# Two transformer blocks on one core: the ends, the passage between the blocks, the pooling products and the order of an FFN's last step rearranged

## The chip, the cores and the metric

The kernel runs on one core of one Trainium2 chip. The metric is the device time of one execution in microseconds (us). The change is judged by the medians of several executions of the two kernels on the same chip.

## What is computed

An input `x` of 256 tokens by 1024 features passes through two stacks of two layers each. All weights are float32.

```python
def first_block(x, mem, ...):
    for l in range(DEPTH):                       # DEPTH = 2
        x = x + 0.5 * swiglu(rms_norm(x, ffn1_norm[l]), ffn1_w_gate[l], ffn1_w_up[l], ffn1_w_down[l])
        x = x + hybrid_mixer(rms_norm(x, mix_norm[l]), w_in[l], ...)
        x = x + memory_cross_attention(rms_norm(x, cross_norm[l]), rms_norm(mem, mem_norm[l]), ...)
        x = x + 0.5 * swiglu(rms_norm(x, ffn2_norm[l]), ...)
    return rms_norm(x, final_norm)

def second_block(x, ...):
    for l in range(DEPTH):
        x = x + swiglu_half(rmsnorm(x, g_ffn1[l]), w1_ffn1[l], w3_ffn1[l], w2_ffn1[l])
        h = rmsnorm(x, g_mix[l])
        q_sb, k_sb, v_sb, q_r, k_r, v_r, g_r, u_p, gate = jnp.split(h @ w_in[l], split_points, axis=-1)
        y_sb, y_ret = stick_breaking_attention(q_sb, k_sb, v_sb), retention(q_r, k_r, v_r, g_r)
        y_pool = pool_mixer(u_p, w_pool[l], pool_scale[l])
        merged = gates[:, :, 0] * (y_sb @ w_branch_sb[l]) + gates[:, :, 1] * (y_ret @ w_branch_ret[l]) \
            + gates[:, :, 2] * (y_pool @ w_branch_pool[l])
        x = x + merged @ w_out[l]
        x = x + swiglu_half(rmsnorm(x, g_ffn2[l]), w1_ffn2[l], w3_ffn2[l], w2_ffn2[l])
    return rmsnorm(x, g_final)
```

`swiglu(h) = (silu(h @ w_gate) * (h @ w_up)) @ w_down` with 2816 hidden features. The kernel writes the 256x1024 result as its only output.

## The kernel before

**Split products.** A float32 product is made of three passes in the float32r format. Every weight tile is split by ScalarE (ACT) into a rounded part `whi` (`split_hi`) and by VectorE (DVE) into the rest `wlo` (`split_lo`); the activations, transposed on TensorE (PE) against the identity matrix `ident` (`turn_piece`), are split in the same way into `hT_hi` and `hT_lo` (`turn_out` on ACT and on DVE). `split_product` then issues three matmuls.

**Units.** All weights pass as 1 MB units through a ring of three slots (`raw`, `whi`, `wlo`). SyncE (SP) loads unit u+3 into a slot once DVE has made `wlo` of unit u; ACT rounds unit u+3 once PE has finished unit u. One such unit is 24 matmuls with 512 columns (or their like), so PE, DVE and ACT move through the program in step, each in its own written order. The order of every engine is written out by hand, with semaphores between them.

**The FFN.** `ffn` works in 11 steps of 256 hidden features: two units of gate and up weights, one unit of down weights. The first step is made for tokens as rows (`tokens_unit`), the following by `wide_unit`; the last `down` uses `last_aT`. In the last step ACT rounds the next stage's first unit (`off + FFN_UNITS`) before it evaluates silu and rounds the product. The FFN's result is added to the residual `xres` in four pieces (piece i is token half i % 2 and feature half i // 2) by DVE: `add_and_norm` adds a piece (`add`), multiplies it with the gain of the next norm (`gained`, giving `xn`), and in between makes the rests of the first two transposed pieces (`turn_out`) that the next stage's first unit needs. There are eight FFNs; after seven of them such a stage follows.

**Norms.** The reciprocal root of the mean square is applied later, so the squares (`squares` on ACT, then a root on ACT and a reciprocal on DVE) run beside the next stage's first products. Between the blocks there are two norms one behind the other: `gain_final`, `joint_squares` and `final_scale` compute both, while the products already run on `x` times both gains.

**Branches of block 1.** Behind the 22 units of `w_in_2` PE transposes the retention output of each token half (`r_yT`), and between the two does the small products of the pooling mixer with `w_pool` (`pool_groups`, into PSUM bank 2). ACT and DVE turn that result into a split operand (`p_hi`, `p_lo`). Before the first branch unit (`B_BR`, stick-breaking) PE waits for `s_lo` and for `p_lo`:

```python
pe.wait_ge(s_lo, l + 1)
pe.wait_ge(p_lo, l + 1)
tall_unit(1, l, B_BR, from_hT(0), 0, True, True)
```

DVE multiplies each branch output with its gates; for the last branch (units `B_BR + 2` and `+ 3`) this goes by pieces, and the pieces of `xn` feed the output projection `B_OUT`.

**Ends.** At the start the ACT queue loads a gain row, two pieces of `x`, `ident`, two more pieces; SP loads the first unit in two halves and then whole units. PE spreads the gain row over 128 partitions by two matmuls (one bank of 512 columns each), DVE multiplies (`first_piece`), PE transposes, and the first unit begins. At the end `last_output` (DVE) and `last_norm` (ACT) make the final norm; DVE scales all four pieces, and the last is stored from the ACT queue.

## Time and profile before

| | |
|---|---|
| time, median of 3 executions | 2411.71 us (2410.25 to 2413.52) |
| the profiled execution's own time | 2411.78 us |
| its span, first to last instruction | 2410.0 us |
| TensorE busy | 2387.7 us, 99% of the span, 13060 matmul records |
| TensorE weight loads busy | 2056.7 us, 85% |
| VectorE, ScalarE, GpSimd busy | 1541.1, 1198.1, 66.4 us |
| HBM read | 425.60 MB, 177 GB/s over the span |
| mean granted TensorE clock | 0.999 |

Busy time of TensorE is that of pipelined matmuls whose ends are modelled: it tells where PE is not idle, and the spacing of the starts tells the speed. The granted clock is 1.00 at 2.4 GHz and 0.50 at 1.2 GHz. For the first microseconds the column prints 1.00 although the spacing of the matmuls is that of the lower level; there the spacing tells the level.

### The profile page before, as it was taken

How to read it: one execution, taken by the hardware profiler on the slowest of the kernel's cores; microseconds unless marked ns; L12 is line 12 of the kernel's file. 1: busy time of each engine (PE TensorE's matmuls, PEld its weight loads, DVE VectorE, ACT ScalarE, POOL GpSimd, SP SyncE). 2: the span in 40 equal slices, each digit the busy share in tenths (PEclk: the TensorE clock that was granted, in tenths of full speed). 3: DMA queues.
4: the chain of work that ended last, by engine and by line, in shares of the span. 5: the costliest groups of instructions: out<-in, count | busy, mean ns of one | idle time of the engine just before them, and what ended most of it. 6: DMA issues, size and time to landing. Idle time of an engine off the chain costs nothing.

```text
span 2410.0 us, 33389 instructions
## 1 busy us (share of the span) xinstructions
PE 2387.7 (99%) x13060; PEld 2056.7 (85%) x13060; DVE 1541.1 (64%) x1392; ACT 1198.1 (50%) x1196; POOL 66.4 (3%) x46
## 2 busy tenths in 40 slices
PE   9999999999999999999999999999999999999998
PEld 7888889888888898898888888878888888887887
DVE  6667855566666686556667666457666667457666
ACT  5447554444544475445445445555445445554543
POOL 0000410000000023000000000000000000000000
PEclk9999999999999999999999999999999999999999
DMA  8555434465565563436556556535555556544653
GB/s 287 192 191 175 139 123 166 143 195 192 174 204 191 173 190 109 140 131 199 186 192 209 192 191 192 168 138 184 192 191 186 194 187 197 179 157 148 206 181 119
DMA packets 328855, 427.92 MB, mean 178 GB/s; under 512 B 15489, under 2 KB 294273, under 8 KB 328514
## 3 DMA queue, kind: packets, MB, share of 16 engines
q1 hardware_dynamic: 324368, 411.94, 53.1%
q10 hardware_dynamic: 4402, 14.76, 1.7%
q8 instruction: 64, 1.05, 0.2%
q14 instruction: 21, 0.17, 0.0%
HBM read 425.60 MB, written 1.05 MB: 177 GB/s over the span
## 4 chain that ended last, share of the span: by engine, by line
PE 89%; DVE 6%; ACT 3%; issue 2%; POOL 0%; DMA 0%; ACTq 0%; DVEq 0%
PE ps L975 24%; PE ps L922 15%; PE ps L923 15%; PE ps L924 15%; PE ps L979 13%; DVE wlo L1469 1%; PE ps L935 1%; ACT whi L486 1%; PE ps L1147 1%; DVE xn L1492 1%; DVE xres L1529 1%; PE ps L1299 1%; PE ps L1279 1%; ACT arena L500 0%; DVE arena L1765 0%
## 5 line engine op out<-in xcount | busy, mean ns | idle before, releaser
L1469 DVE TENSOR_TENSOR wlo<-raw,whi 128x2048 fp32r<-128x2048 f32 x393 | 897.0, 2284 | 515.1 <-ACT whi L486 515.0
L486 ACT ACTIVATE whi<-raw 128x2048 fp32r<-128x2048 f32 x393 | 748.7, 1905 | 600.4 <-PE ps L924 373.0
L975 PE MATMUL ps<-hT,whi 128*128 128x512 f32 x2560 | 610.7, 390 | 0.0
L975 PEld LDWEIGHTS ps<-hT,whi 128*128 128x128 f32 x2560 | 474.9, 188 | 95.1
L922 PE MATMUL ps<-whi,hT 128*128 128x512 f32 x928 | 374.4, 403 | 6.8 <-DVE hT L1520 4.1
L924 PE MATMUL ps<-whi,hT 128*128 128x512 f32 x928 | 363.9, 392 | 0.0
L923 PE MATMUL ps<-wlo,hT 128*128 128x512 f32 x928 | 363.0, 391 | 0.0
L979 PEld LDWEIGHTS ps<-hT,wlo 128*128 128x128 f32 x2560 | 329.3, 191 | 13.1
L979 PE MATMUL ps<-hT,wlo 128*128 128x256 f32 x2560 | 333.3, 283 | 0.0
L922 PE MATMUL ps<-whi,aT_hi 128*128 128x512 f32 x640 | 250.0, 391 | 0.0
L923 PE MATMUL ps<-wlo,aT_hi 128*128 128x512 f32 x640 | 249.9, 391 | 0.0
L924 PE MATMUL ps<-whi,aT_lo 128*128 128x512 f32 x640 | 249.0, 389 | 0.0
L922 PEld LDWEIGHTS ps<-whi,hT 128*128 128x128 f32 x928 | 175.3, 189 | 45.9 <-issue 10.5
L924 PEld LDWEIGHTS ps<-whi,hT 128*128 128x128 f32 x928 | 174.9, 188 | 37.9
L923 PEld LDWEIGHTS ps<-wlo,hT 128*128 128x128 f32 x928 | 175.6, 189 | 33.7 <-issue 0.5
L568 ACT ACTIVATE prod<-ps 128x512 f32<-128x512 f32 x80 | 48.1, 601 | 293.0 <-PE ps L979 293.0
L922 PE MATMUL ps<-hT,whi 128*128 128x256 f32 (+2 forms) x608 | 174.2, 286 | 0.0
L923 PE MATMUL ps<-hT,whi 128*128 128x256 f32 (+2 forms) x608 | 171.6, 282 | 0.0
L924 PE MATMUL ps<-hT,wlo 128*128 128x256 f32 (+2 forms) x608 | 171.5, 282 | 0.0
L1576 DVE TENSOR_REDUCE silu_g<-ps 128x512 f32<-128x1024 f32 x80 | 97.9, 1224 | 90.5 <-PE ps L979 90.5
L924 PEld LDWEIGHTS ps<-whi,aT_lo 128*128 128x128 f32 x640 | 120.2, 188 | 25.6
L922 PEld LDWEIGHTS ps<-whi,aT_hi 128*128 128x128 f32 x640 | 120.5, 188 | 22.9
(262 smaller groups left out, 2031.7 us busy)
## 6 DMA issues: line engine op xcount, KB each, us to landing
raw<-in_w_ffn SPq DMA_DIRECT2D x264, 512.0 KB, 4.3
raw<-in_w_in SPq DMA_DIRECT2D x144, 512.0 KB, 4.8
raw<-in_ffn_w_down SPq DMA_DIRECT2D x88, 512.0 KB, 4.2
raw<-in_ffn_w_up SPq DMA_DIRECT2D x87, 512.0 KB, 4.0
raw<-in_ffn_w_gate SPq DMA_DIRECT2D x87, 512.0 KB, 4.9
raw<-in_w_out SPq DMA_DIRECT2D x32, 512.0 KB, 4.3
gain<-in_gains ACTq DMA_DIRECT2D x16, 512.0 KB
raw<-in_cross_wk SPq DMA_DIRECT2D x16, 512.0 KB, 4.5
```

The lines of the kernel that those rows point to most:

```text
L486: act.activation(whi[:, s, :, 0:cols], raw[:, s, :, 0:cols], ACT.Copy).then_inc(hi_ready, 1)
L568: act.activation(prod[:, :, :], ps[:, G + 2:G + 4, SEQ:2 * SEQ], ACT.Copy).then_inc(up_rest, 1)
L922: pe.matmul(out, l_hi, r_hi, start=first, stop=False, skip_group_check=True)
L923: pe.matmul(out, l_hi, r_lo, start=False, stop=False, skip_group_check=True)
L924: return pe.matmul(out, l_lo, r_hi, start=False, stop=last, skip_group_check=True)
L935: mm = pe.transpose(ps[:, banks[t], k * P:(k + 1) * P], piece(xn, i)[:, k * P:(k + 1) * P], ident[:, :])
L975: pe.matmul(ps[:, G + n, :], whi[:, s, k, n * P:(n + 1) * P], both[k], start=first and k == 0, stop=False, skip_group_check=True)
L979: mm = pe.matmul(ps[:, G + n, 0:SEQ], wlo[:, s, k, n * P:(n + 1) * P], both[k][:, 0:SEQ], start=False, stop=last and k == 3, skip_group_ch ...
L1147: mm = pe.matmul(ps[:, bank + g // 4, g % 4 * P:(g % 4 + 1) * P], a[:, g * P:(g + 1) * P], c[:, g * P:(g + 1) * P], start=True, stop=True)
L1279: mm = pe.matmul(ps[:, TR + h % 2, t * SEQ:(t + 1) * SEQ], q[:, at + t * P:at + (t + 1) * P], k_[:, at:at + SEQ], start=(k == 0), stop=(k ...
L1469: dve.tensor_tensor(wlo[:, s, :, 0:cols], raw[:, s, :, 0:cols], whi[:, s, :, 0:cols].bitcast(F32), ALU.subtract).then_inc(lo_ready, 1)
L1576: dve.tensor_reduce(silu_g[:, :, :], ps[:, G:G + 2, :].rearrange("p n (v c) -> p n c v", v=2), AX, ALU.add).then_inc(gate_sum, 1)
```

## The change

The two kernels compute the same. What differs:

- **Start.** `ident` is loaded from the POOL queue; ACT loads two pieces of `x`, SP the two others, between the first and the second unit. The second unit comes in halves too, and the splits of both units go by halves or quarters (`FIRST_PARTS`). PE multiplies a tile of ones (`busy`) 9 times before the first gain matmul and 3 times behind it; the second gain matmul follows the first transposed piece, and the first unit starts on the `hi` parts alone. DVE makes `xn` of pieces 1 to 3 between its splits.
- **End.** The product with the gain of one piece goes to POOL, the scaling of two pieces to ACT, and the stores follow each piece.
- **Passage between the blocks.** The squares of `x` run between the turns, both roots are taken in one ACT instruction, `xres` is scaled (`final_scale`) after the third weight split.
- **Pool groups.** The small products move into the first branch unit, behind its second piece, and to bank 4; the wait for `p_lo` moves behind that unit.
- **Turns.** In `add_and_norm`, and in the last branch, `turn_out` of pieces 0 and 1 each stand one piece earlier.
- **FFN's last step.** ACT does silu and the rounding of the product before it rounds the next stage's first unit.

```diff
+BUSY = (9, 3)
+        FIRST_PARTS = {(0, 0): (slice(0, 2),), (0, 1): (slice(2, 3), slice(3, 4)), (1, 0): (slice(0, 2),), (1, 1): (slice(2, 4),)}
...
@@ SP: the first two units @@
-                        if b == l == off == k == 0:
+                        if b == l == off == 0:
+                            if k:
+                                xt = x[0].rearrange("(t p) d -> p t d", p=P)
+                                for i in range(TB, PIECES):
+                                    sp.dma_start(piece(xres, i), piece(xt, i)).then_inc(x_loaded[i], 16)
                             for half in range(2):
...
@@ POOL: first and last instruction @@
+            pool.dma_start(ident[:, :], eye).then_inc(ident_loaded, 16)
...
+            pool.wait_ge(x_ready, seen + 3)
+            pool.tensor_tensor(piece(xn, i), piece(xres, i), gain[:, 0:512], ALU.mult).then_inc(last_side, 1)
...
@@ ACT: squares at the passage @@
+            def block_squares(n, add, t):
+                act.wait_ge(x_ready, PIECES * add + 2 + t + 1)
+                act.activation(sq_junk[:, t * DM:(t + 1) * DM], xres[:, t, :], ACT.Square, accum_out=stat[:, 0, 0, t:t + 1]).then_inc(sq_sum, 1)
+            def joint_squares(n):
                 for t in range(TB):
+                    act.wait_ge(sq_sum, 2 * n - 2 + t + 1)
+                    act.wait_ge(x_final, 2 + t + 1)
                     act.activation(sq_junk[:, t * DM:(t + 1) * DM], x_gained[:, t, :], ACT.Square, accum_out=stat[:, 1, 0, t:t + 1]).then_inc(sq_sum, 1)
+                act.activation(fin[:, 6:8], ident[:, 0:2], ACT.Sqrt)
+                act.wait_ge(both_sums, 1)
+                act.activation(stat[:, :, 1, :], stat[:, :, 0, :], ACT.Sqrt, scale=1.0 / DM).then_inc(sq_done, 2)
...
+                elif (b, l, e) == (1, 0, 0):
+                    turn_out(T, (0, 1))
+                    split_hi(b, l, off + 2)
+                    block_squares(n, add, 0)
+                    turn_out(T, (2,))
+                    block_squares(n, add, 1)
+                    turn_out(T, (3,))
...
@@ ACT: an FFN's last step @@
                 up_low(FF_STEPS - 1, off + FFN_UNITS - 3)
-                if more:
-                    split_hi(b, l, off + FFN_UNITS)
                 silu(FF_STEPS - 1)
                 round_product(FF_STEPS - 1, off + FFN_UNITS - 3, out=last_aT(hT_hi))
                 if more:
+                    split_hi(b, l, off + FFN_UNITS)
                     split_hi(b, l, off + FFN_UNITS + 1)
...
@@ PE: start @@
+            def keep_busy(n):
+                for i in range(n):
+                    pe.matmul(ps[:, G, i % 4 * P:(i % 4 + 1) * P], busy, busy, start=True, stop=True)
+            keep_busy(BUSY[0])
             pe.wait_ge(gain_loaded, 16)
-            for n, bank in enumerate(GAIN_BANKS):
-                pe.matmul(ps[:, bank, :], ones_row, gain[0:1, n * 512:(n + 1) * 512], start=True, stop=True).then_inc(first_gain, 1)
+            spread_gain(0)
+            keep_busy(BUSY[1])
             pe.wait_ge(ident_loaded, 16)
...
@@ PE: before and in the first branch unit @@
                 def pool_groups():
+                    pe.wait_ge(p_wl, l + 1)
+                    pe.wait_ge(r_lo, TB * l + 1)
...
                 pe.wait_ge(s_lo, l + 1)
+                pe.wait_ge(p_dT, l + 1)
+                tall_unit(1, l, B_BR, from_hT(0), 0, True, True, then={1: pool_groups})
                 pe.wait_ge(p_lo, l + 1)
-                tall_unit(1, l, B_BR, from_hT(0), 0, True, True)
...
@@ DVE: add_and_norm @@
                 for i in range(PIECES):
                     if T is not None and i == PIECES - 1:
+                        turn_out(T, (1,))
+                    add(b, l, j, i, off, factor)
+                    if T is not None and i == PIECES - 2:
                         turn_out(T, (0,))
-                    add(b, l, j, i, off, factor)
-                    if T is not None and i == PIECES - 1:
-                        turn_out(T, (1,))
                     gained(add_no(b, l, j), n, i, joint)
...
@@ DVE: the last branch, by pieces @@
+                    if i >= TB:
+                        turn_out(turn_no(1, l, 2), (i - TB,))
                     if i < PIECES - 1:
                         dve.wait_ge(br_piece, (PIECES - 1) * l + i + 1)
                     else:
-                        turn_out(turn_no(1, l, 2), (0, 1))
                         wait_unit(dve, 1, l, B_BR + 3)
```

**DVE at the end of an FFN.** These are VectorE's rows from the split of the next stage's first unit on; L1529 adds a piece to the residual, L1492 makes `xn`, L1520 makes the rest of a transposed piece. Before:

```order
L1529 SCALAR_TENSOR_TENSOR xres<-ps,stat,xres 128x512

L1492 TENSOR_TENSOR xn<-xres,gain 128x512

L1529 SCALAR_TENSOR_TENSOR xres<-ps,stat,xres 128x512

L1492 TENSOR_TENSOR xn<-xres,gain 128x512

L1529 SCALAR_TENSOR_TENSOR xres<-ps,stat,xres 128x512

L1492 TENSOR_TENSOR xn<-xres,gain 128x512

L1520 TENSOR_TENSOR hT<-ps,hT 128x4x128

L1529 SCALAR_TENSOR_TENSOR xres<-ps,stat,xres 128x512

L1520 TENSOR_TENSOR hT<-ps,hT 128x4x128

L1492 TENSOR_TENSOR xn<-xres,gain 128x512

L1469 TENSOR_TENSOR wlo<-raw,whi 128x2048

```

And in the changed kernel (L1598 adds, L1555 makes `xn`, L1589 makes the rest):

```order
L1598 SCALAR_TENSOR_TENSOR xres<-ps,stat,xres 128x512

L1555 TENSOR_TENSOR xn<-xres,gain 128x512

L1598 SCALAR_TENSOR_TENSOR xres<-ps,stat,xres 128x512

L1555 TENSOR_TENSOR xn<-xres,gain 128x512

L1598 SCALAR_TENSOR_TENSOR xres<-ps,stat,xres 128x512

L1589 TENSOR_TENSOR hT<-ps,hT 128x4x128

L1555 TENSOR_TENSOR xn<-xres,gain 128x512

L1589 TENSOR_TENSOR hT<-ps,hT 128x4x128

L1598 SCALAR_TENSOR_TENSOR xres<-ps,stat,xres 128x512

L1555 TENSOR_TENSOR xn<-xres,gain 128x512

L1532 TENSOR_TENSOR wlo<-raw,whi 128x2048

```

The first rest moved ahead of the third piece's `xn`, and the second rest ahead of the fourth piece's addition.

**PE at the start.** TensorE's first rows, before: two gain matmuls, two transposed pieces, then the first unit's triples.

```order
L917 MATMUL ps<-gain,prod 128x512 x2
L935 MATMUL ps<-ident,xn 128x128 x8
L922 MATMUL ps<-whi,hT 128x512
L923 MATMUL ps<-wlo,hT 128x512
L924 MATMUL ps<-whi,hT 128x512
```

In the changed kernel (L953 is the tile of ones times itself, L958 a gain matmul, L981 a transposed piece):

```order
L953 MATMUL ps<-arena 128x128 x9
L958 MATMUL ps<-gain,prod 128x512
L953 MATMUL ps<-arena 128x128 x3
L981 MATMUL ps<-ident,xn 128x128 x4
L958 MATMUL ps<-gain,prod 128x512
L1005 MATMUL ps<-whi,hT 128x512 x2
L1008 MATMUL ps<-wlo,hT 128x512 x2
L1011 MATMUL ps<-whi,hT 128x512 x2
L981 MATMUL ps<-ident,xn 128x128 x4
```

The second gain matmul and the second transposed piece moved behind the first piece, and the first six products stand by kind instead of in triples.

**PE at the branches.** TensorE's rows at the first branch unit; L1444 transposes the retention output, L1432 is the pool product. Before:

```order
L924 MATMUL ps<-whi,hT 128x512

L1444 MATMUL ps<-ident,arena 128x128 x4

L1432 MATMUL ps<-arena,wpool_l 64x256 x4

L1444 MATMUL ps<-ident,arena 128x128 x4

L922 MATMUL ps<-whi,hT 128x512

L923 MATMUL ps<-wlo,hT 128x512

L924 MATMUL ps<-whi,hT 128x512

L922 MATMUL ps<-whi,hT 128x512

```

In the changed kernel (L1508 transposes, L1499 is the pool product); between the two pieces lie the 12 products of the unit's first half:

```order
L1508 MATMUL ps<-ident,arena 128x128 x8
L968 MATMUL ps<-whi,hT 128x512
...
L970 MATMUL ps<-whi,hT 128x512
L1499 MATMUL ps<-arena,wpool_l 64x256 x4
L968 MATMUL ps<-whi,hT 128x512
L969 MATMUL ps<-wlo,hT 128x512
```

The pool products moved from between the transposes into the branch unit.

## Rows read from the trace of the kernel before

**Rows 1.** Page: span, busy time, and the splits (busy, mean ns | idle)
```profile
span 2410.0 us, 33389 instructions
PE 2387.7 (99%) x13060; PEld 2056.7 (85%) x13060; DVE 1541.1 (64%) x1392; ACT 1198.1 (50%) x1196; POOL 66.4 (3%) x46
...
L1469 DVE TENSOR_TENSOR wlo<-raw,whi 128x2048 fp32r<-128x2048 f32 x393 | 897.0, 2284 | 515.1 <-ACT whi L486 515.0
L486 ACT ACTIVATE whi<-raw 128x2048 fp32r<-128x2048 f32 x393 | 748.7, 1905 | 600.4 <-PE ps L924 373.0
```

**Rows 2.** Who waited for whom, TensorE: total us, times, longest
```profile
PE ps L922 <- DVE hT L1520: 4.1, 8, 0.7
PE ps L922 <- issue: 2.6, 2, 1.3
PE ps L1080 <- DVE prod L1563: 1.1, 1, 1.1
```

**Rows 3.** Timeline of the start: start us, us, engine, line, operation [idle before <-releaser]
```profile
2.29 3.75 PE L917 MATMUL ps<-gain,prod 1*128 1x512 f32 x4 [2.29 <-DMA gain<-in_gains]
5.69 0.69 DVE L1681 TENSOR_TENSOR xn<-xres,ps 128x512 f32<-128x512 f32 x1 [4.60 <-DMA xres<-in_x]
7.87 1.97 PE L935 MATMUL ps<-ident,xn 128*128 128x128 f32 x8 [1.83 <-DMA ident<-in_eye]
10.49 0.76 PE L922 MATMUL ps<-whi,hT 128*128 128x512 f32 x1 [0.65 <-DVE hT L1520]
...
24.24 3.59 PEld L975 LDWEIGHTS ps<-hT,whi 128*128 128x128 f32 x16
```

**Rows 4.** Windows: length, busy us (matmuls) by engine, PEclk, DMA share, GB/s
```profile
10.49:14.89 4.40, 4.40 (x10) 3.44 (x11) 3.32 (x5) 2.84 (x2) 0.00 (x0) 1.00 1.10 348
1608.60:1612.10 3.50, 3.50 (x9) 2.69 (x10) 2.68 (x2) 3.47 (x4) 0.00 (x0) 0.54 0.00 0
2172.10:2176.00 3.90, 3.77 (x17) 3.14 (x18) 2.91 (x3) 3.87 (x4) 0.00 (x0) 1.00 0.00 0
```

**Rows 5.** Timeline, end of the first FFN: ACT, DVE and PE
```profile
195.75 0.60 ACT L543 ACTIVATE hT<-ps 128x512 fp32r<-128x512 f32 x1 [2.54 <-PE ps L935]
196.61 0.69 DVE L1492 TENSOR_TENSOR xn<-xres,gain 128x512 f32<-128x512 f32 x1
197.22 0.68 DVE L1520 TENSOR_TENSOR hT<-ps,hT 128x512 fp32r<-128x512 f32 x1
198.05 0.47 PE L922 MATMUL ps<-whi,hT 128*128 128x512 f32 x1 [0.52 <-DVE hT L1520]
```

**Rows 6.** Timeline, passage between the blocks: ACT
```profile
1284.77 1.06 ACT L500 ACTIVATE arena<-xres 128x1024 f32<-128x1024 f32 x1 [0.27 <-issue]
```

**Rows 7.** Timeline, around the first branch unit of block 1
```profile
1606.65 0.84 ACT L860 ACTIVATE hT<-ps,pscale_l 128x256 fp32r<-128x256 f32 x2 [0.42 <-PE ps L1432]
1607.52 0.88 DVE L1999 SCALAR_TENSOR_TENSOR hT<-ps,pscale_l,hT 128x256 fp32r<-128x256 f32 x2 [0.57 <-ACT hT L860]
1608.49 0.47 PE L922 MATMUL ps<-whi,hT 128*128 128x512 f32 x1 [1.31 <-issue]
...
1615.84 2.36 DVE L2006 TENSOR_TENSOR xn<-ps,arena 128x1024 f32<-128x1024 f32 x2 [3.75 <-PE ps L924]
1628.15 0.69 DVE L2034 TENSOR_TENSOR arena<-ps,arena 128x512 f32<-128x512 f32 x1
1634.43 0.51 PE L922 MATMUL ps<-whi,hT 128*128 128x512 f32 x1
```

**Rows 8.** Timeline of the end, and the multiply on POOL by line
```profile
2403.24 0.74 DVE L1654 SCALAR_TENSOR_TENSOR xres<-ps,stat,xres 128x512 f32<-128x512 f32 x1
2404.78 0.29 ACT L529 ACTIVATE sst<-sst 128x1 f32<-128x1 f32 x1
2406.91 0.36 ACTq L532 DMA_DIRECT2D out<-xres  x1
...
L469 POOL TENSOR_TENSOR xn<-arena x4: 1301/1314/1321, 319.1 to 952.6; 128x512 f32<-128x512 f32 x4
```

239 lines of the change are left out of this document (141 added, 98 removed).

## Prediction

> **What bounds the kernel now.** I read the page first: TensorE is busy 2387.7 of 2410.0 us [rows 1], so its own work is nearly the whole time, and this change takes no product away. What an edit can give is PE's idle time (22.3 us) and time at the lower clock. Next I read whom PE waited for [rows 2]: eight waits for DVE's rest of a transposed piece (4.1 us, of which 0.65 at the start, so 3.5 in seven FFN ends), two of 1.3 us with no releaser named, one of 1.1 us for the first product of an FFN; then the timeline at each of these places, at the start, and at the end. The reader is to see in them which engine finishes last, and what it did just before. As to the clock, ten matmuls of 512 columns take 4.40 us after the first starts at 10.49, but 17 take 3.77 us later [rows 4]: 0.44 us each at 1.2 GHz, 0.23 at 2.4. The same slow pace stands behind the wait at 1608.49, where the granted clock is 0.54 over 3.5 us, though not behind its twin near 2172 (1.00).
>
> **Sum.** Durations are of the profiled execution: span 2410.0, own time 2411.78 (1.8 more), 0.07 above the median of 2411.71. I sum against 2411.78.
>
> *FFN ends, seven times.* PE finishes the second transposed piece and then needs the first piece's rest. ACT has rounded that piece at 196.35, but DVE makes `xn` of the third piece first (196.61), so the rest starts at 197.22 and PE at 198.05 after 0.52 us idle [rows 5]. In the new order the rest takes the slot at 196.61 and ends at 197.29, before PE is free at 197.53. The third piece's `xn` ends 0.7 later, at 197.98, and PE wants it only 12 products on (12 x 0.23 = 2.8, at 200.3). The second piece's rest now waits on DVE for ACT (about 198.2), and behind it are queued the last addition, the last `xn` (about 200.3, not 199.7) and the next split; their users come at 203 and later. So all of the seven waits goes: **-3.5**. Bounds: -2.0, if a third of each comes back through ACT's piece, and -3.5.
>
> *Silu and rounding ahead of the next weights.* The product is ready some 1.5 us sooner, yet PE does not idle for it: no such wait stands in [rows 2]. The next unit's rounding (1.9 us [rows 1]) moves behind the product's, but DVE takes up its rest after the product's anyway, and PE turns to that unit at 197.5 only. The cover is PE's last two units (48 x 0.23 = 11 us). **0.**
>
> *Passage between the blocks.* ACT does four squares in a row from 1284.77 (1.06 each), two roots and a table load, so silu and the product on DVE come late, and PE waits 1.1 us [rows 2, 6]. Two squares (2.1 us) move into ACT's idle time between the turns, one root instruction goes, and the DVE instruction of 1.4 us that scales `xres` stands later. The product then comes some 2.5 us sooner, against 1.1 needed: **-1.1** (bounds -0.5 and -1.1).
>
> *Pool groups, twice.* Between the transposes and the first branch product now lies the chain pool products, ACT (two at 1606.65, 0.84 together), DVE (1607.52, 0.88), and PE starts at 1608.49 after 1.3 us idle [rows 7]. After the change PE goes on at about 1606.0, and pool products run in the middle of the unit; ACT's evacuation comes behind its sigmoid, about 1610.6, and DVE's ends at 1611.5, before PE is through with the unit (1606.0 + 24 x 0.23 + 0.9 = 1612.4). This wait is covered. But the splits are late next: ACT's takes 1.9 and DVE's 2.3 us [rows 1], so DVE's for the third unit starts only at 1612.5 and its gate product at 1614.8, 2.4 us behind PE, where it now starts at the moment PE is done (1615.84). The following DVE work is as long as PE's, so the lag stays: the first `xn` piece, now begun at 1628.15, would begin at 1626.2 with PE ready for the last unit at 1623.2. PE would wait 0.3 us for it and 0.5 us for the second rest ahead of the output projection. The turns put one piece earlier help here: in the old order the second of these would be 1.1. From the idle time, the two transfers between kinds of matmul (0.5) and these 0.8 us: 1.0 saved each, **-2.1** (bounds: -0.4, if PE waits for the gate product too, and -3.6, if DVE's lag costs nothing). The slow stretch adds to it: 9 matmuls too long by 0.2 us, 1.8 us, once in this execution [rows 4]. PE has no idle time ahead of it any more, so I take **-1.8** (bounds 0 and -1.8).
>
> *Start.* Ones run from about 1.4 us. A gain matmul of 512 columns takes 3.75 / 2 = 1.9 us at the lower clock [rows 3], a tile of 128 columns a quarter, 0.45: nine fill until 5.4 us at the lower level and less if the clock rises among them. If it rises at about 5, the gain row is spread by 5.9 and piece 0's `xn` (its load lands by 5.6 [rows 3]) by 6.7; transposing, the second gain matmul (0.95) and ACT's rounding bring the first product to 8.3 instead of 10.49. From there to the end of the second unit lie 48 x 0.23 = 11.0, three transposed pieces (1.1) and waits: 0.2 for a quarter of the weights and about 0.9 for the fourth piece, since DVE does a weight split and a rest before its `xn`. That gives 21.5 against 24.24: -2.7. If the clock rises only at the end of the fillers, all is 1.4 later: -1.3. I take the middle, **-2.0**. If it does not rise before the products, ones and both gain matmuls at 1.2 GHz bring the first product to about 11.7: +1.5, the other bound. `ident` from POOL has no row; from ACT's queue, behind two 256 KB pieces, it was waited for until 7.87 [rows 3]. By the nearest rows it is between the gain row's landing (2.3) and 7.9, and is wanted at 6.7: I take 0; at worst 1.2.
>
> The Trainium skill ("TensorE: Matmul & The Clock Gate", Part 1) says that how many matmuls run at the lower level at a start differs between executions of one kernel. By that page the terms of the clock, here 1.8 and half of 2.0, would not be in every execution, and a median could hold none of the 1.8. The two branch stages above, one slow and one not, agree.
>
> *End.* Behind the last addition (2403.24) come a square and a root (2404.78 to 2405.07), then DVE alone scales four pieces, and the last store is issued at 2406.91 [rows 8]. After: ACT scales piece 0 before that square, DVE one piece before the root; behind the root stand a reciprocal (0.2), then ACT's scaling (0.6) beside DVE's last, and the store at about 2406.0: **-0.9**. The piece multiplied on POOL takes 1.3 us there [rows 8], 2402.7 to 2404.0, and is wanted at 2405.3. Bounds: -0.4 (POOL or a table late by half a us) and -1.0.
>
> "SBUF — State Buffer" ("Who interferes with whom") of the Trainium skill says that a DVE instruction with two SBUF inputs and a POOL instruction that reads SBUF exclude each other. DVE's last gain product would then wait for POOL's, by that page some 0.3 us if POOL starts late: -0.6 instead of -0.9. No row here shows the two together.
>
> Sum: -3.5 - 1.1 - 2.1 - 1.8 - 2.0 - 0.9 = -11.4: 2411.8 - 11.4 = **2400.4**.
>
> **Rivals.**
> 1. *The ones do not raise the clock* (or `ident` is late): start +1.5 instead of -2.0, 2403.9. For it: the transposes and gain matmuls before 10.49 did not raise it. Against: they had 1.8 us of idle time among them, the ones have none. 16 in 100.
> 2. *The clock term of the branch does not count,* because the executions behind the median did not have the slow stretch, or the new one falls into one: 2402.2. For it: one stage of two shows it. Against: the profiled time is the median's. 16 in 100.
> 3. *The waits move instead of going.* DVE's lag in the branches costs more than 1.3 us each, and at the FFN ends the rest of the second piece, which now holds up the last addition, stalls PE: only passage, end and start are left, 2411.8 - 4.0 = 2407.8, or nothing. For it: DVE is 64% busy and its order at these places is full. Against: the slack of 0.2 us at 197.3 and of 2 us behind it. 5 in 100.
> 4. *Slower: the next weights come late.* The rounding that moved behind silu and product (ACT, last FFN step) delays the next unit's rest. Its price is seven times what it is late beyond PE's need. The rest ends at about 193.0 now, and PE needs it at 197.5, so it decides from a delay of 4.5 us; to be slower by 4.8 us it would have to be 6.8 us late. I get none. 2 in 100: above 2416.
>
> **How the numbers follow.** The likeliest (61 in 100) is the sum with the clock risen among the ones: 2400.4, own range 2398.3 (no lag, -2.7 at the start) to 2402. Rivals 1 and 2 reach to 2403.9, so the range is **2397.8 to 2404.3**; rivals 3 and 4 and the smaller sums lie outside, under 2 in 10. A measurement of this kernel can tell about 0.2% (4.8 us) from no change. Faster by more than that (below 2406.9): the first three cases, 93 in 100; same 4; slower 3.
>
> **What would show it.** No wait for a rest at the seven FFN ends, none of 1.1 us between the blocks; the first branch product right behind the transposes with a granted clock of 1.00, and new waits of 0.3 and 0.5 us behind the last branch; the second unit's end at 21 to 23 us and a matmul spacing of 0.23 from the first product on; the last store issued 2.8 us behind the start of the last addition, not 3.7. The prediction is wrong if the spacing at the start stays at 0.44 us, if the waits in the branches add up to over 2 us, or if a split waits for the moved rounding.

## The result, and the profile after

The changed kernel takes 2397.36 us (median of 4 executions, 2397.06 to 2399.36), the kernel before in the same comparison 2411.14 (2410.25 to 2413.52): ratio 0.9942, 95% interval 0.9929 to 0.9954. The forecast was 2400.4 us with a range of 2397.8 to 2404.3: the direction is right, the time is 0.44 us under the range. Ten more executions of the changed kernel, made with the experiments, lie between 2397.08 and 2402.65; the median of all 14 is 2399.23.

The profiled execution took 2397.38 us (before 2411.78), with a span of 2395.2 (before 2410.0). From the page of the profile and the list of who waited for whom, TensorE:

```profile
span 2395.2 us, 33468 instructions
PE 2383.9 (100%) x13084; PEld 2057.0 (86%) x13084; DVE 1541.4 (64%) x1392; ACT 1200.8 (50%) x1199; POOL 68.4 (3%) x48
```
```profile
PE ps L1212 <- DVE arena L1848: 2.9, 4, 0.9
PE ps L953 <- DVE arena L1758: 1.3, 1, 1.3
PE ps L981 <- DVE xn L1765: 0.6, 1, 0.6
```

The three lines of [rows 2] are gone. The first line here was there before too, at the same length; the others are the wait for the ones to be written and one wait at the start. Timeline of the start (answers to [rows 3]):

```profile
1.29 3.91 PE L953 MATMUL ps<-arena 128*128 128x128 f32 x18 [1.29 <-DVE arena L1758]
5.13 1.12 PE L958 MATMUL ps<-gain,prod 1*128 1x512 f32 x2
6.43 0.69 DVE L1765 TENSOR_TENSOR xn<-xres,ps 128x512 f32<-128x512 f32 x1 [5.19 <-PE ps L958]
7.26 0.63 PE L981 MATMUL ps<-ident,xn 128*128 128x128 f32 x4
16.48 0.66 PE L981 MATMUL ps<-ident,xn 128*128 128x128 f32 x4 [0.61 <-DVE xn L1765]
22.44 3.79 PE L1039 MATMUL ps<-hT,whi 128*128 128x512 f32 x16
```

The first gain matmul (recorded as two rows, 5.13) takes 1.12 us; at the lower level it takes 2.07 (experiment 2). So the clock had risen while the ones ran. The second unit ends at 22.44 instead of 24.46. End of the first FFN, ACT, DVE and PE (answers to [rows 5]):

```profile
193.73 0.60 ACT L565 ACTIVATE hT<-ps 128x512 fp32r<-128x512 f32 x1 [2.54 <-PE ps L981]
194.36 0.69 DVE L1589 TENSOR_TENSOR hT<-ps,hT 128x512 fp32r<-128x512 f32 x1 [0.19 <-ACT hT L565]
194.91 0.60 PE L981 MATMUL ps<-ident,xn 128*128 128x128 f32 x4
195.26 0.48 PE L968 MATMUL ps<-whi,hT 128*128 128x512 f32 x1
```

The rest now follows ACT's rounding at once, and the first product starts 0.35 us after the start of the transposes' row, with no wait. Passage between the blocks (to [rows 6]), and the first branch unit (to [rows 7]):

```profile
1279.76 1.06 ACT L525 ACTIVATE arena<-arena 128x1024 f32<-128x1024 f32 x1 [0.91 <-DVE arena L1563]
1287.76 0.75 DVE L1632 SCALAR_TENSOR_TENSOR prod<-ps,silu_g 128x256 f32<-128x256 f32 x2
1289.36 0.60 PE L1144 MATMUL ps<-ident,prod 128*128 128x128 f32 x4
```
```profile
1598.33 0.48 PE L968 MATMUL ps<-whi,hT 128*128 128x512 f32 x1
...
1603.26 0.88 DVE L2081 SCALAR_TENSOR_TENSOR hT<-ps,pscale_l,hT 128x256 fp32r<-128x256 f32 x2 [3.17 <-ACT hT L895]
1605.07 2.29 DVE L1532 TENSOR_TENSOR wlo<-raw,whi 128x2048 fp32r<-128x2048 f32 x1 [0.93 <-ACT whi L497]
1607.27 2.35 DVE L2088 TENSOR_TENSOR xn<-ps,arena 128x1024 f32<-128x1024 f32 x2
```

The product is ready at 1288.51, 0.85 us before PE takes it; the branch unit starts right behind the transposes. The end (to [rows 8]):

```profile
2389.13 1.27 POOL L483 TENSOR_TENSOR xn<-xres,gain 128x512 f32<-128x512 f32 x1 [1439.76 <-DVE xres L1727]
2389.53 0.75 DVE L1727 SCALAR_TENSOR_TENSOR xres<-ps,stat,xres 128x512 f32<-128x512 f32 x1 [0.24 <-PE ps L970]
2391.07 0.29 ACT L548 ACTIVATE sst<-sst 128x1 f32<-128x1 f32 x1
2392.34 0.36 ACTq L554 DMA_DIRECT2D out<-xres  x1
```

From the last addition to the last store's issue it is 2.81 us instead of 3.67.

**Where the 14.8 us of span went.** I followed the start times of the same PE instructions (rows of the norms' transposes and of the FFN products' transposes) through both traces and took the differences between neighbours:

| place | forecast | measured |
|---|---|---|
| start | -2.0 | -2.02 |
| seven FFN ends | -3.5 (0.50 each) | -5.17 (0.71 to 0.77 each) |
| four ends of attention parts, same code | none | -0.68 (0.17 each) |
| passage | -1.1 | -1.00 |
| branch stages, without a slow stretch | -2.1 (1.05 each) | -3.08 (1.54 each) |
| slow stretch of before | -1.8 | -1.56 |
| end | -0.9 | -1.25 |
| sum | -11.4 | -14.8 |

The time outside the span grew from 1.78 to 2.18 us, so the own time fell by 14.4.

### The profile page after: what moved, and what is told of

Its sections match the earlier page's. It is cut to its first block, busy times and chain, and to the rows that moved or that the text cites. A ratio compares the mean times of both kernels' runs of the same rounds, so it can differ in the third digit from the quotient of the medians.

```text
span 2395.2 us, 33468 instructions
## 1 busy us (share of the span) xinstructions
PE 2383.9 (100%) x13084; PEld 2057.0 (86%) x13084; DVE 1541.4 (64%) x1392; ACT 1200.8 (50%) x1199; POOL 68.4 (3%) x48
## 3 DMA queue, kind: packets, MB, share of 16 engines
HBM read 425.60 MB, written 1.05 MB: 178 GB/s over the span
## 4 chain that ended last, share of the span: by engine, by line
PE 93%; DVE 3%; ACT 2%; issue 1%; POOL 0%; ACTq 0%; DVEq 0%
PE ps L1039 24%; PE ps L968 16%; PE ps L969 16%; PE ps L970 16%; PE ps L1043 13%; PE ps L981 2%; DVE wlo L1532 1%; PE ps L1212 1%; ACT whi L497 1%; PE ps L1364 1%; PE ps L1344 1%; DVE arena L1848 0%; PE ps L1420 0%; ACT arena L511 0%; PE ps L1267 0%
```

## The experiments

The starts of the same PE instructions (milestones) are compared with the two traces above; they repeat to some 0.05 us. Line numbers can differ by up to four where an edit adds or drops lines.

**1. Only the order of the rests**, in the kernel before.

```
                 for i in range(PIECES):
                     if T is not None and i == PIECES - 1:
-                        turn_out(T, (0,))
+                        turn_out(T, (1,))
                     add(b, l, j, i, off, factor)
-                    if T is not None and i == PIECES - 1:
-                        turn_out(T, (1,))
+                    if T is not None and i == PIECES - 2:
+                        turn_out(T, (0,))
```

> The kernel before with one edit: in the last addition and gain product of a part, DVE takes the first turned piece's rest after the third addition and the second piece's rest ahead of the fourth addition. Theory: a late rest costs PE the time from the start of one stage to the start of the next, not the idle time that the list of waits shows. Before, the first product behind the transposes at 196.93 started 1.12 us after them, an undisturbed one 0.36 us after its transposes. So each of the seven FFN ends gives 0.76 us (5.3), and the six other places with the same code, where no wait is listed, 0.54 - 0.36 = 0.18 us each (1.1): 6.4 us, 2405.3 from the profiled 2411.8. Rival 1, the prediction's term: only the listed idle time goes, 0.5 us at each of seven, 3.5 us, 2408.3, and nothing at the six others. Rival 2: the 0.24 us beyond the listed wait that the changed kernel gained at each FFN end come from silu and rounding standing earlier; then this kernel gains 0.52 at each and still nothing elsewhere, as in rival 1, but the next kernel loses 0.24 at each.

Measured: 2405.6 us against 2411.69, ratio 0.9975 (0.9965 to 0.9984). In the profiled execution the seven FFN ends gave 0.66 to 0.74 us each, 5.0 in all, and the four attention ends and the output projection's end in each layer of block 1 0.16 to 0.22 each. Its own start was 1.5 us later than that of before, and neither branch stage had a slow stretch. So the theory holds; in the total, the late start and the missing slow stretch happen to cancel. Rival 1, the forecast's term, is too small by a third: a listed wait of 0.52 us was a loss of 0.76. Rival 2 falls too, since silu and rounding are at their old place here. Why the list shows too little can be read in the row of the transposes ahead of the wait of [rows 5], in the kernel before:

```profile
196.93 0.60 PE L935 MATMUL ps<-ident,xn 128*128 128x128 f32 x4
```

The wait of 0.52 us is counted from the end of this row (197.53), and a row lasts longer than the time to the next start. From start to start it is 1.12 us (196.93 to 198.05), while in the trace after, transposes of 0.60 us are followed by a product 0.35 us after their start. Every place where a product follows late hides some 0.25 us more than is listed, and where the delay is shorter than that, nothing is listed at all: that is what the attention ends lost.

**2. Silu and rounding behind the next weights again**, in the changed kernel, in two runs.

```
                 up_low(FF_STEPS - 1, off + FFN_UNITS - 3)
+                if more:
+                    split_hi(b, l, off + FFN_UNITS)
                 silu(FF_STEPS - 1)
                 round_product(FF_STEPS - 1, off + FFN_UNITS - 3, out=last_aT(hT_hi))
                 if more:
-                    split_hi(b, l, off + FFN_UNITS)
                     split_hi(b, l, off + FFN_UNITS + 1)
```

> The changed kernel with one part undone: in an FFN's last step ACT rounds the next weights ahead of silu and of the product's rounding, as before. Theory, and the prediction: this order is worth nothing where the turned pieces' rests are in time, since PE has two units of work (11 us) in front of it; every milestone within 0.05 us of the changed kernel, 2397.4. Rival 1: it carries 0.24 us of each FFN end, 1.7 us in seven: 2399.1. Rival 2: silu and product would be late for PE's last units without it: a wait of up to 1.5 us (the time by which they come sooner) in each of seven: up to 2408.

> The same kernel as in the run before with silu and rounding behind the next weights, again, now timed in rounds: its 5.3 us lay at the start alone, where the pace of the products stayed at 0.43 us up to 17 us. Theory: when the clock rises at the start differs from one execution to the next, with ones too, and the order of silu costs nothing; most executions at 2397 to 2399 like the changed kernel, now and then one near 2402.8. Rival 1: this kernel's start is always late: median 2402.8. Rival 2: the changed kernel's start is as uncertain as this one's, and its own four executions were lucky: a median between, 2399 to 2402.

Measured: 2402.77 us in the first run; median 2402.61 of five (2399.66 to 2402.95) in the second. Behind the start nothing differs: the FFN ends give 0.69 to 0.74 us each, at most 0.03 less than in the changed kernel, 0.1 us in all. The edit costs nothing, as forecast. The 5.3 us lie ahead of the second unit's end (27.74 instead of 22.44). PE's timeline of the first run:

```profile
1.29 4.21 PE L954 MATMUL ps<-arena 128*128 128x128 f32 x18 [1.29 <-DVE arena L1759]
5.42 2.07 PE L959 MATMUL ps<-gain,prod 1*128 1x512 f32 x2
11.86 1.22 PE L1006 MATMUL ps<-whi,hT 128*128 128x512 f32 x2
15.87 0.63 PE L970 MATMUL ps<-wlo,hT 128*128 128x512 f32 x1
```

The same ones, from the same time on, without a gap behind them, and the pace stays at 0.43 us for 512 columns (1.2 GHz) up to 17 us. This is the first rival of the forecast, down to the first product (11.7 there, 11.86 here).

**3. The changed kernel again**, unchanged, twice, five rounds each.

> The changed kernel itself, again, in five rounds. Eight profiled executions so far show three kinds of start: the products' pace rises to 0.23 us each at about 4.7 us (the changed kernel and one other), at about 12.3 us (four, one of them without ones) or after 15 us (two with ones), at 22.4, 24.4 and 27 us for the end of the second unit. Theory: the 2397.4 of the changed kernel was a median of mostly early ones, and which kind comes is not the kernel's doing: five more executions have several at 2399.4 and 2402.7, and the median lies at 2399 or more, inside the range that was predicted. Rival: the early rise is this kernel's own, and the others lost it by their small shifts of code or loads: four or five of the executions at 2397.1 to 2397.5.

> The changed kernel a third time, in five rounds. Theory: of its nine executions so far three were at 2397.1 to 2397.4, three at 2399.2 to 2399.4 and three at 2402.3 to 2402.7; five more fall at the same three places, and the median of all 14 lies at 2399 to 2400, against 2397.4 in the first four. Rival: the late kind belonged to the chip of the second timing, and here all are at 2397 to 2399.4.

Measured: median 2402.34 (2399.22, 2399.23, 2402.34, 2402.38, 2402.65), and 2397.39 on another chip (2397.08, 2397.21, 2397.39, 2399.45, 2399.56). With the first four: six at 2397.1 to 2397.4, five at 2399.2 to 2399.6, three at 2402.3 to 2402.7. My description of the middle kind in the expectation was wrong: I had seen only that its products speed up at 12.3. Windows of the start of the first of these runs (length, busy us of PE, PEld, DVE, ACT, POOL, granted clock, DMA share, GB/s), and of the run of experiment 8:

```profile
5.50:9.30 3.80, 3.65 (x14) 1.69 (x14) 2.26 (x3) 2.12 (x4) 0.00 (x0) 0.95 1.00 346
9.40:12.20 2.80, 2.80 (x8) 2.12 (x8) 1.95 (x4) 0.47 (x1) 0.00 (x0) 0.50 1.10 354
12.60:16.00 3.40, 3.35 (x18) 2.46 (x16) 2.42 (x3) 1.54 (x2) 0.00 (x0) 1.00 1.10 348
```
```profile
9.40:12.20 2.80, 2.80 (x6) 0.96 (x5) 1.70 (x4) 1.63 (x3) 0.00 (x0) 1.00 1.10 354
```

In the middle kind the clock rose too (the first gain matmul took 1.13 us at 5.43), and from 9 to 12 us the granted clock fell to half. In the late kind the granted clock reads 1.00 while the products run at the slow pace. So there are three starts: risen early and kept; risen early and halved for some 3 us; not risen before 16 to 20 us. The traces with the twelve ones, other edits included, order them by the moment of the rise. In the three profiled executions that kept it, the first gain matmul ran wholly at the upper level (1.12 us) from 4.90, 5.01 and 5.13 on. In the seven that began it at 5.42 or 5.43 and had a rise, it took 1.13 to 1.44 us, so the rise came at its start or within it, and the granted clock fell back in all seven. (In experiment 11 an early rise was followed by a fall too, while PE waited.)

**4. No ones**, in the changed kernel, in two runs (`BUSY = (0, 0)`).

> The changed kernel without the 12 products of ones (18 and 6 rows in the profile) ahead of the first gain products. Theory: they raise TensorE's clock before the kernel's own products. Without them PE starts with the gain row at about 2.5 us, but the clock stays at 1.2 GHz through the gain products and transposes, and rises only among the products: ten or more matmuls of 512 columns at 0.44 instead of 0.23 us (2.1 us or more), less what the idle PE gives back by starting the gain product sooner (0.5 us at most, since piece 0 lands at 5.5 us either way): the end of the second unit 1.5 to 2.5 us later than 22.44. Rival 1: the gain of 2.0 us at the start comes from the loads in halves, the piecewise order and ident alone: 22.4 within 0.3 us. Rival 2: the clock rises in the first 2 us of products anyway and loads bound the start: 0.3 to 1.0 us later.

> The changed kernel without its products of ones, again, in five rounds. Theory: without ones the early rise at 4.7 us cannot happen, the other two kinds of start remain: executions at 2399.3 and about 2402, none at 2397.4, and a median 0 to 2 us above that of the changed kernel in the same rounds, by how many early ones that has. Rival 1: the ones do nothing: the same mixture as the changed kernel, medians within 0.3 us. Rival 2: the ones keep the clock down in some executions (they make the late kind likelier), and this kernel is the faster by 1 to 3 us in the median.

Measured: 2399.34 us; then median 2399.76 of five (2399.15 to 2399.96), beside the changed kernel's 2402.34 in the same rounds. The pace rose at 12.7 and at 14.5 us, with the granted clock at 1.00 throughout. No early kind, as the theory says; but the median is 2.6 us below the changed kernel's, as the second rival of the later run had it (against the 14 executions' median of 2399.23 it is 0.5 above). All six lie within 0.8 us, against 5.6 us for the 14 with ones.

**5. Pool groups between the transposes again**, in the changed kernel.

```
                 for t in range(TB):
+                    pe.wait_ge(r_y, l + 1)
+                    if t == 0:
+                        pe.wait_ge(p_dT, l + 1)
+                        pe.wait_ge(p_wl, l + 1)
                     for k in range(4):
                         mm = pe.transpose(...)
                     mm.then_inc(r_yT, 1)
+                    if t == 0:
+                        pool_groups()
                 pe.wait_ge(s_lo, l + 1)
-                tall_unit(1, l, B_BR, from_hT(0), 0, True, True, then={1: pool_groups})
                 pe.wait_ge(p_lo, l + 1)
+                tall_unit(1, l, B_BR, from_hT(0), 0, True, True)
```

(shortened), with bank 2 and ACT's and DVE's instructions back at their old places.

> The changed kernel with the pool groups as before: their products between the two transposes ahead of the first branch product, in bank 2, ACT and DVE taking them out ahead of the second piece, and PE waiting for DVE's rest. DVE's turned pieces in the last branch stay one piece earlier. Prediction's step: 1.8 us of wait and changes between kinds of matmul come back, but DVE's lag of 0.8 us, which it paid for the later splits, goes: 1.0 to 1.05 us slower in each of two layers. Theory after the traces: DVE's lag cost nothing (no wait behind the last branch), so 1.3 to 1.5 us come back in each layer, and 1.5 us more wherever the wait is followed by products at 1.2 GHz. Rival: the gain in this part came from the turned pieces in the last branch alone, and this kernel is within 0.3 us of the changed one in each layer.

Measured: 2401.75 us, from an early start (second unit's end at 22.3). The first layer loses 1.46 us, the second 3.0; the windows around the two first branch units show why:

```profile
1603.50:1607.00 3.50, 3.50 (x18) 2.88 (x17) 1.34 (x2) 1.53 (x4) 0.00 (x0) 1.00 0.41 97
2161.60:2165.00 3.40, 3.40 (x8) 2.64 (x9) 2.58 (x2) 3.37 (x4) 0.00 (x0) 0.52 0.00 0
```

1.46 us is the idle time, in both, and 1.55 the slow stretch, which this time stands in the second layer [rows 4] (in before it stood in the first; in experiment 1 in neither). All 1.3 us of the listed wait were gained and a little more, and the 0.8 us that the forecast took off for DVE's lag do not belong to the pool groups: what PE loses behind the last branch (experiment 6) is the same here.

**6. The turned pieces of the last branch in the old order**, in the changed kernel.

```
                 for i in range(PIECES):
                     h, t = divmod(i, 2)
-                    if i >= TB:
-                        turn_out(turn_no(1, l, 2), (i - TB,))
                     if i < PIECES - 1:
                         dve.wait_ge(br_piece, (PIECES - 1) * l + i + 1)
                     else:
+                        turn_out(turn_no(1, l, 2), (0, 1))
```

> The changed kernel with DVE's turned pieces in the last branch as before: both rests of the first two pieces ahead of the fourth piece of the sum, instead of one ahead of the third and one ahead of the fourth. Prediction's step: the second of the two waits would be 1.1 instead of 0.5 us, 0.6 us in each layer. Theory after the traces: the first product of the output projection (1622.30) needs the first piece's rest, which ends at 1622.1; behind the third piece's two instructions and ahead of the fourth's it would end at 1623.5, so PE waits 1.2 us in each layer, 2.4 us in all: 2399.8. Rival: PE is not ready for it that early or makes up for it at the fourth piece's transposes: 0 to 0.3 us.

Measured: 2400.72 us from a middle start, 0.70 us more in each layer. The wait, behind the last branch's transposes:

```profile
1625.38 0.47 PE L968 MATMUL ps<-whi,hT 128*128 128x512 f32 x1 [0.87 <-DVE hT L1589]
```

So the rests do come late in the old order, and this part of the change covers it: 0.6 had been forecast for it, and my 1.2 after the trace was too much. From start to start the first product loses 1.12 us here. But the new order has a wait of its own, which no list shows. PE's rows in the changed kernel, and DVE's second rest:

```profile
1623.54 0.40 PE L970 MATMUL ps<-whi,hT 128*128 128x512 f32 x1
1624.05 0.50 PE L968 MATMUL ps<-whi,hT 128*128 128x512 f32 x1
1624.39 0.39 PE L969 MATMUL ps<-wlo,hT 128*128 128x512 f32 x1
```
```profile
1623.32 0.68 DVE L1589 TENSOR_TENSOR hT<-ps,hT 128x512 fp32r<-128x512 f32 x1
```

Between undisturbed products lie 0.23 us, here 0.51 and 0.34: 0.4 us are lost, right behind the second rest's end. With both rests ahead of the fourth piece this gap is gone, so 0.7 is left of the 1.12. Of the 0.8 us of waits that the forecast had in spite of the new order, the 0.3 did not come; the 0.5 for the second rest did, as 0.4, in both layers.

**7. The squares of the passage behind the turned pieces**, in the changed kernel (ACT's two `block_squares` moved down to just ahead of `joint_squares`).

> The changed kernel with the passage's two squares of the unscaled xres behind the turned pieces, as before, instead of between them; the joint root and the later scaling of xres stay. The prediction said that the squares save ACT 2.1 us and the product comes 2.5 us sooner against 1.1 needed: by that 0.7 us of wait come back. Theory after the trace: ACT stands idle for 0.91 us ahead of the squares of the gained xres (waiting for DVE, 1279.76), so 1.2 of the 2.1 us reach the product, which is ready 0.85 us before PE takes it (1288.51 against 1289.36): 0.3 to 0.5 us of wait. Rival: the passage's gain came from the two squares alone and the joint root gave none: all 1.0 us comes back.

Measured: 2400.25 us from a middle start. PE waits 0.45 us for the product, and the passage together with the FFN end ahead of it gives 1.17 instead of 1.75 us: 0.58 comes back. The squares' place is thus worth over half of the passage's 1.0; that the joint root and the later scaling give the rest follows by subtraction, neither was tried alone. Again the loss is more than the wait.

```profile
1292.20 0.66 PE L1143 MATMUL ps<-ident,prod 128*128 128x128 f32 x4 [0.45 <-DVE prod L1631]
```

**8. xn of the fourth piece one place earlier** at the start, in two runs: an attempt at a better version.

```
                     first_split_lo(1, 0)
+                    first_piece(3)
                     turn_out(T, (2,))
-                    first_piece(3)
```

> The changed kernel with one instruction moved: at the start DVE makes xn of the fourth piece right behind the first two quarters' rest of the second unit, at 14.05, where it stood idle for 1.09 us, instead of behind the rest of the third piece. Theory: the only wait that PE still has between its first product and the end of the second unit, 0.61 us at 15.87, goes, and nothing is behind it: 0.6 us, 2396.8. Rival: it makes the third piece's rest 0.1 to 0.6 us late where the fourth piece's load or ACT's rounding is later than in the profile, and part of the gain goes back: 0 to 0.4 us.

> The changed kernel with the fourth piece's xn one place earlier, again, beside the changed kernel in the same rounds. Theory: its executions come in the same kinds as the changed kernel's, each 0.6 to 0.8 us sooner (2396.5, 2398.6, 2401.6 against 2397.3, 2399.3, 2402.4), by the wait of 0.61 us that is gone; which median is the lower in five rounds is decided by the kinds that come up, and may be either's. Rival: the edit also changes how often each kind comes.

Measured: the wait at 15.87 is gone. First 2396.47, 2398.55, 2398.57, 2398.71, 2401.52; then five at 2401.34 to 2401.79, in the rounds in which the changed kernel had 2397.39. At equal start each is 0.7 to 0.9 us sooner than the changed kernel (its late ones 2401.5 against 2402.4). But all five of the second run were of the late kind, so its median was 4.1 us longer. PE's timeline there starts like that of experiment 2:

```profile
5.43 2.07 PE L958 MATMUL ps<-gain,prod 1*128 1x512 f32 x2
11.86 1.22 PE L1005 MATMUL ps<-whi,hT 128*128 128x512 f32 x2
```

Up to the first product nothing that the edit touches has run on PE, DVE or ACT, so the edit cannot have caused it in the program's order. Executions of one run often share a kind (five late of five here, four of five in experiment 2); what sets the moment of the rise, and with it the kind, stays open.

**9. The identity from ACT's queue**, in the changed kernel.

> The changed kernel with the identity loaded from ACT's queue behind the first two pieces of x, as before, instead of from POOL's. Theory: there it lands at 7.87 (before's row), 0.6 us behind the time at which PE wants it now (7.26): the first product at 9.5 instead of 8.87, and the second unit's end 0.3 to 0.6 us later (part is hidden, since PE waits for the fourth piece anyway). Rival: it was late before because a transfer from POOL frees nothing and the queue was full of x; with x's last pieces on SP's queue it lands in time, and nothing changes (within 0.1 us).

Measured: 2401.33 us. PE waits for the identity, and the slow stretch after the early rise then lasts 6.8 us (granted clock 0.50 from 9.2 to 16), so the total is not comparable; the wait is:

```profile
8.73 0.69 PE L981 MATMUL ps<-ident,xn 128*128 128x128 f32 x4 [1.15 <-DMA ident<-in_eye]
```

The theory's sign is right, its size twice as much: 1.2 us. POOL's queue brings the identity in time, which had no row in the forecast.

**10. The end's POOL multiplication on DVE**, in the changed kernel.

> The changed kernel with the end's multiplication of the third piece on DVE (between the reciprocal and the last addition) instead of on POOL. Theory: it takes 0.69 us from 2389.28 on, where DVE has 0.24 us idle ahead of the last addition at 2389.53: that starts 0.4 us later, and so does all behind it: 0.4 us. Rival 1 (POOL and DVE take turns at SBUF, so that POOL's piece cost DVE time): the instructions of DVE around it get shorter by up to 0.3 us, and the net is 0.1 us or nothing. Rival 2: DVE's order is not what the end waits for, since ACT's square of the first piece stands beside it: 0.

Measured: 2399.40 us from a middle start; 0.26 us more from the second layer's last FFN to the end of the span, where the theory had 0.4. DVE's gain products take the same 0.67 to 0.69 us in both kernels, so rival 1 is not seen. It was hardly tried: in the changed kernel POOL's multiplication and DVE's gain product overlap for 0.1 us only (2390.31 against 2390.40). The exclusion that the Trainium skill ("SBUF — State Buffer", "Who interferes with whom") states, and that the forecast weighed, cannot be told from that; no run here had a longer overlap at this place. Yet the time outside the span was 1.80 us, as in the run without the transfer from POOL (1.83), against 2.11 to 2.21 in each of the 54 executions that have both.

**11. The identity first on ACT's queue, ahead of x,** with the edit of 8: a second attempt.

> The changed kernel with two edits of the start: xn of the fourth piece one place earlier (0.6 to 0.8 us at equal pace), and the identity loaded from ACT's queue between the gain row and x instead of from POOL's. Theory: the time outside the span (own time less span), 2.1 to 2.2 us in 40 executions of kernels with both the transfer from POOL and the multiplication on POOL at the end, but 1.8 in the one without that transfer and in the one without that multiplication, falls to 1.8: 0.35 us. The identity, 64 KB, lands well ahead of 7 us; x's first pieces land some 0.5 us later (one more issue of 0.5 us on ACT's queue), 6.0 instead of 5.5, which is hidden where the pace stays slow (the first piece is wanted at 6.4) and costs up to 0.3 us where it rises early. Sum: 1.0 us less than the changed kernel at equal start: 2396.3, 2398.3 or 2401.4. Rival 1: the two single looks at 1.8 were chance: 2.15 stays, 2396.6, 2398.6 or 2401.7. Rival 2: x's delay is paid in full behind ACT's queue: 0.5 us later, no gain over the kernel with the fourth piece alone.

Measured: 2401.73 us (2400.94 to 2401.98). The time outside the span is 1.78 to 1.88 in all five: that part of the theory holds, 0.35 us. But x is not 0.5 us late, it is 3:

```profile
8.69 0.69 DVE L1765 TENSOR_TENSOR xn<-xres,ps 128x512 f32<-128x512 f32 x1 [7.46 <-DMA xres<-in_x]
9.52 1.08 PE L981 MATMUL ps<-ident,xn 128*128 128x128 f32 x4 [2.70 <-DVE xn L1765]
```

It began at 6.43 in the changed kernel, and x's first piece landed at 5.5. The attempt failed, and neither the theory nor a rival had 3 us. With the transfer ahead of x went another order of landings: the first weights' half came 1.1 us sooner than in the changed kernel (ACT rounds it from 4.73 on instead of 5.83). What delayed x was not separated. The clock fell as well: risen among the ones, it stands at 0.50 from 7.6 on, while PE waits for x, up to 17.8 us.

**12. A lean start, with none, twelve and four products of ones**, all with the edit of 8 and the second gain matmul behind piece 1's transposes.

```
                     turn_piece(0, T0, 0)
-                    spread_gain(1)
...
                         turn_piece(b, T, 1)
+                        spread_gain(1)
```

> A version of the changed kernel with a lean start: no ones; the second half of the gain row is spread behind piece 1's transposes instead of ahead of the first products; xn of the fourth piece one place earlier (as in the run on the fourth piece). Theory: without ones the start has no late kind (six executions: 2399.2 to 2400.0); the second gain product, 2.0 us at the slow pace right ahead of the first weight product at 9.2, is what that waits for there, so the products start at 8.0, 1.2 us sooner, and the fourth piece gives 0.6: 2397.5 to 2398.5, in a narrow band, 1 us or more below the changed kernel's executions without an early rise. Rival 1: the loads bound the start (the second half of the first weights lands at 8.3 to 8.7): 0.3 us in all, 2399.3. Rival 2: products that start 1.2 us sooner only run 1.2 us longer at the slow pace, since the rise comes at the same time whatever PE does: half of the gain, 2398.7.

> The same version with the ones as in the changed kernel (9 and 3). Theory (the ones keep the late kind alive): the same three kinds, each 0.6 to 1 us below the changed kernel's 2397.3, 2399.3 and 2402.5, so a spread of over 4 us and a median above that of the version without ones, if late ones are as frequent as so far (10 of 25). Rival: whether the start is late has nothing to do with the ones (it was chance that none of six executions without them was late): then the version without ones shows late executions too, and this one is the faster by the early kind.

> The same version with four products of ones ahead of the first gain product and none behind it: they end at about 3.1 us, when the gain row lands, so PE has no idle time up to the end of the first gain product at 5.2 and about 1 us ahead of the first transposes. Theory: what makes the late kind is PE's unbroken work from 1.3 us on without a rise; with a pause behind it the start is as without ones, 2397.5 to 2398.5, none near 2401.5. Rival 1: any ones at 1.3 us do it: late executions as with all 12. Rival 2: an early rise comes as often as with 12 (5 of 25) and no late one: the fastest of the three versions.

Measured: none 2400.58 (2398.54, 2398.76, 2400.58, 2400.80, 2401.10); twelve 2399.24 (2397.25, 2399.17, 2399.24, 2400.91, 2403.66); four 2400.92 (2398.28 to 2402.17). My theory that the ones bring the late kind fell: without ones the pace rose at 16.9 us in the profiled execution, so late rises come without them too (in experiment 1, which has no ones either, it rose at 17.2). The second rival to the version with none, 2398.7, fits two of the five; in the other three the slow pace lasted longer still. The first product of the profiled one starts at 7.98 instead of 9.21:

```profile
7.98 1.22 PE L1005 MATMUL ps<-whi,hT 128*128 128x512 f32 x2 [0.69 <-ACT hT L565]
16.42 0.63 PE L968 MATMUL ps<-whi,hT 128*128 128x512 f32 x1
16.85 0.49 PE L969 MATMUL ps<-wlo,hT 128*128 128x512 f32 x1
```

The means of the five are 2399.96, 2400.05 and 2400.48, the spreads 2.6, 6.4 and 3.9 us: the ones widen the spread, and with five executions each no gain in the mean is seen. My theory for four ones (2397.5 to 2398.5) failed as well.

## Why the prediction was right or wrong

**FFN ends: the step that failed.** The forecast took "all of the seven waits" and sized them by the listed idle time, 3.5 us. They gave 5.17, and four more places with the same code, which the forecast did not have since no wait is listed, gave 0.68 (the two output projections' ends another 0.4, counted with the branches). Experiment 1 shows that the order of the rests alone does it. The bounds (-2.0 to -3.5) excluded the truth, and these 2.3 us are more than the 0.44 by which the range was missed. The mechanism was right, and the cover behind it too: nothing queued behind the rests was waited for.

**Silu and rounding: right.** Experiment 2: 0.1 us in seven.

**Passage: right** (1.1 against 1.0), though through less than forecast: the product comes 1.8 us sooner and not 2.5, since DVE's pieces of `x` times the gain made ACT wait 0.91 us; it is still 0.85 us ahead of need. Start to start PE gains 1.3 us at the product and loses some 0.2 ahead of it, at 1280.92, where the fourth piece's rest now stands behind those pieces.

**Pool groups: mechanism right, size too small by 1.0.** The chain of 1.3 us left the path. In each layer PE gained 1.5 us at the first branch unit (1.8 forecast), lost 0.1 to 0.2 net behind the last branch (0.8 forecast) and gained 0.2 at the output projection's end (nothing forecast). Of the two waits behind the last branch the one of 0.3 did not come; the one of 0.5 came as 0.4, unlisted, of which 0.1 was there before. DVE's split for the third unit began at 1605.07, 0.3 us before PE was through with the unit (ACT's next instruction, which waits for it, starts at 1605.38), not 0.1 behind, so its gate product stood 1.9 us behind PE instead of 2.4. Of the 1.0, 0.4 is again the order of the rests, at the two output projections' ends. The measured -3.08 lies within the bounds, nearer to -3.6 than to the -2.1 taken.

**Slow stretch: 1.56 where 1.8 was taken.** That it is not in every execution holds: of three profiled executions with the old place, one had it in the first layer, one in the second, one in neither. So it comes in part of the executions, and rival 2 was a fair case; none of the 17 profiled executions with the new place has it.

**Start: the number was right in the profiled execution (-2.02), by luck, and it is no constant.** The middle was taken between two cases of the clock. In the changed kernel and those with the same start the three kinds put the second unit's end at 22.2 to 22.4, 24.3 to 24.7 or 27.7 us (before: 24.46 and, in experiment 1, 25.97). The early rise itself had been put at -2.7 (the second unit's end at 21.5), and gave -2.02 (22.44): PE took up the first piece at 7.26 and not at 6.7, and the first product came at 8.87 and not at 8.3. So the middle of the two cases fits without either case being right. (The 24.24 that the forecast counted from is the weight load's row; the matmul of the same place starts at 24.46.) Three of the first four executions were early ones, by their times. Over 14 the median is 2399.23, within the range. That does not excuse the FFN term: the forecast's sum had the start of the early kind already (-2.0), so the excess is elsewhere. Rival 1 had the late kind's first product right (11.7 against 11.86); that kind came in 3 of 14. Its total (2403.9 against 2402.4) is near by luck: it priced this start at +1.5, but with the slow pace lasting up to 17 us it was +3.3 (27.74 against 24.46), and the 3.4 us that the rest of the sum lacked more than made up for that.

The Trainium skill ("TensorE: Matmul & The Clock Gate", Part 1) says that the number of matmuls at the lower level at a start is run-variable. By that rule the start's term is not one number. The traces agree: with the same ones, the gain matmul at 4.90 us ran at the upper level in one execution, and in another the pace rose only at 20 us (experiments 3 and 12).

**End: 0.35 us more than the -0.9.** 0.86 is the shorter tail behind the last addition, as worked out; 0.16 is the last addition's start, since the multiplication on POOL frees DVE ahead of it (0.26 in experiment 10); the rest lies in the last store's landing.

**Not foreseen: the time outside the span,** +0.36 to 0.4 us. Experiments 9, 10 and 11 tie it to POOL having both its transfer and its multiplication; either taken away gives it back. Why two small things cost this only together was not found.

So the sum was short by 3.4 us of span: 2.35 at the ends of parts, 1.0 in the branches and 0.35 at the end, less 0.25 of the slow stretch and 0.1 of the passage.

## What to carry to other kernels

Size a wait by start to start against an undisturbed twin of the same place, not by the idle time in a list: the list counts from the row's end, and hid 0.17 to 0.25 us at each of 13 places here, six of them altogether, as well as the new order's own wait behind the last branch. Move the rest that TensorE needs next ahead of work that it needs 2 us later, and ask what then covers the work that was put behind it. Time a change to a kernel's start in many executions and by kinds; products of ones ahead of the first weights are no gain by themselves, if the clock rises late all the same or falls again.
